# One step of a hybrid decoder: the input projection in another tile order, small steps set between its tiles, the short convolution moved from GpSimd to VectorE

## What is computed

```
x = LN1(alpha*x + 0.5*SwiGLU_a(x))
z = x @ w_in + b_in        # split: conv B, C, h (512 each) | q (512) | kv_cmp, kv_sel, kv_win (256 each) | gates (24)
y_conv = B * conv3(C * h)                       # causal, depthwise, width 3; samples start from state_conv
o = g0*o_cmp + g1*o_sel + g2*o_win              # compressed, selected and window attention, gates g = sigmoid
x = LN2(alpha*x + concat(o, y_conv) @ w_out)
x = LN3(alpha*x + 0.5*SwiGLU_b(x))
```

## Time and profile before

| | us |
|---|---|
| median of 3 runs (lowest, highest) | 1405.66 (1404.45, 1406.14) |
| the profiled execution | 1405.21 |
| its span, first to last instruction | 1403.5 |
| TensorE busy in the span | 1297.5 (92%) |
| VectorE busy | 749.5 (53%) |
| ScalarE busy | 435.4 (31%) |
| GpSimd busy | 280.9 (20%) |
| mean granted clock of TensorE | 0.968 of 2.4 GHz |

### The profile page before, as it was taken

One profiled execution on the slowest core, in us unless ns is written; L12 is line 12 of the kernel. 1 busy time (PEld: TensorE's weight loads), 2 busy tenths in 40 slices (PEclk: granted clock), 3 DMA queues, 4 the chain that ended last, 5 costly groups with the idle time before them and its releaser, 6 DMA issues.

```text
span 1403.5 us, 30051 instructions
## 1 busy us (share of the span) xinstructions
PE 1297.5 (92%) x11917; PEld 1181.4 (84%) x11917; DVE 749.5 (53%) x1178; ACT 435.4 (31%) x814; POOL 280.9 (20%) x272
## 2 busy tenths in 40 slices
PE   6999999999999889999779999497999999999996
PEld 5999999999999779999546666396899999999995
DVE  3686487477748763221546666646444444444446
ACT  3222223132222244222135565314522122222214
POOL 0342044023314312082344332000000000000000
PEclk9999999999999999999789999698999999999999
DMA  4786267246536402331676674131533333323311
GB/s 136 202 225 175 82 176 210 66 132 197 161 92 183 137 24 76 90 90 34 136 256 226 213 239 136 39 89 54 161 106 105 105 104 104 97 85 102 104 60 64
DMA packets 215978, 178.04 MB, mean 127 GB/s; under 512 B 22995, under 2 KB 206466, under 8 KB 215236
## 3 DMA queue, kind: packets, MB, share of 16 engines
q1 hardware_dynamic: 209732, 159.84, 39.2%
q0 software_dynamic: 6144, 16.79, 3.5%
HBM read 172.63 MB, written 8.10 MB: 129 GB/s over the span
## 4 chain that ended last, share of the span: by engine, by line
PE 76%; DVE 12%; ACT 5%; DMA 3%; issue 3%; SPq 1%; POOL 0%; DVEq 0%; ACTq 0%
PE ps L763 44%; PE ps L890 8%; PE ps L817 7%; PE ps L787 4%; DVE dlo L1670 3%; PE ps L1215 2%; DVE glo L1665 2%; DMA w1p<-in_cmp_w_dram 2%; DMA draw<-in_ffa_down_dram 1%; PE ps L1251 1%; PE ps L1186 1%; PE ps L1231 1%; DVE x L1741 1%; ACT ghi L1331 1%; PE ps L1173 1%
## 5 line engine op out<-in xcount | busy, mean ns | idle before, releaser
L763 PE MATMUL ps<-xh,ghi 128*128 128x272 f32 x1904 | 402.0, 293 | 26.2 <-DVE xl L1935 15.7
L763 PE MATMUL ps<-xl,ghi 128*128 128x272 f32 x1904 | 396.4, 290 | 0.0
L763 PE MATMUL ps<-xh,glo 128*128 128x272 f32 x1904 | 394.1, 288 | 0.0
L763 PEld LDWEIGHTS ps<-xh,ghi 128*128 128x128 f32 x1904 | 305.3, 190 | 43.0 <-issue 24.2
L763 PEld LDWEIGHTS ps<-xl,ghi 128*128 128x128 f32 x1904 | 302.0, 190 | 0.0
L763 PEld LDWEIGHTS ps<-xh,glo 128*128 128x128 f32 x1904 | 301.4, 190 | 0.0
L1665 DVE TENSOR_TENSOR glo<-graw,ghi 128x1024 fp32r<-128x1024 f32 x119 | 155.5, 1307 | 107.1 <-ACT ghi L1331 104.9
L696 POOL COPY perm<-landing 128x1024 f32<-128x1024 f32 x64 | 141.0, 2222 | 303.8 <-DMA landing<-in_cache_cmp_kv_dram 303.7
L1741 DVE SCALAR_TENSOR_TENSOR x<-ps,x 128x544 f32<-128x544 f32 x176 | 126.7, 720 | 107.1 <-PE ps L817 106.7
L1800 DVE SCALAR_TENSOR_TENSOR yt<-ps,yt 128x512 f32<-128x512 f32 x88 | 60.6, 691 | 156.6 <-PE ps L890 156.6
L1331 ACT ACTIVATE ghi<-graw 128x1024 fp32r<-128x1024 f32 x119 | 124.8, 1050 | 34.0 <-PE ps L763 30.7
(11 more groups left out here) (335 smaller groups left out, 1478.6 us busy)
## 6 DMA issues: line engine op xcount, KB each, us to landing
landing<-in_cache_cmp_kv_dram SPq DMA_DIRECT2D x256, 128.0 KB, 2.5
page<-in_cache_sel_kv_dram SPq DMA_DIRECT2D x128, 128.0 KB, 4.9
page<-in_cache_sel_kv_dram POOLq DMA_DIRECT2D x128, 128.0 KB, 5.2
graw<-in_ffa_gate_dram SPq DMA_DIRECT2D x22, 512.0 KB, 4.7
graw<-in_ffa_up_dram SPq DMA_DIRECT2D x22, 512.0 KB, 4.4
draw<-in_ffa_down_dram SPq DMA_DIRECT2D x88, 128.0 KB, 2.7
graw<-in_w_in_dram SPq DMA_DIRECT2D x44, 256.0 KB, 3.3
graw<-in_ffb_gate_dram SPq DMA_DIRECT2D x22, 512.0 KB, 3.9
```

What stands on the lines that cost most here:

```text
L763: last = nc.tensor.matmul(out[:, h, 0:HALF], a[:, k, :], b[:, k, h * HALF:(h + 1) * HALF], start=(k == 0 and a is hi and b is xhi), stop=( ...
```

## The change

The projection's tiles are taken in the order keys and values, q, gates, C and h, B. The small steps are made into functions and called on TensorE between the tiles (some in the middle of a tile, behind its fourth chunk, `middle`), and the other engines' programs are set in the matching order; the loops over tiles are written out. `w1p` and its loads go: L1082's step reads `w1`, and the buffers are laid out so that only the convolution's tiles lie over it. The convolution runs on VectorE, one tile of 128 channels at a time, with fused multiply-adds; `conv_ready` is raised once for each of four. GpSimd issues its pages of sample 0 when the last tile is over, as SP does. The gate products' operand `gate_sel` lies in the window buffers, so window loads 0 and 1 wait for these products and come behind the pages of sample 0. In the second feed-forward layer `token_stores` stands ahead of the wait for the norm, and ScalarE waits for these stores before it writes `yt`, which now lies over `kvtok`.

```diff
+ORDER = (*range(ZC + 4, ZC + 10), *range(ZC, ZC + 4), ZC + 10, *range(4, ZC), *range(4))
+AT = {t: (j % 2, j // 2 + 1) for j, t in enumerate(ORDER)}
...
-        w1p = sb("w1p", [128, 2, HD, HD], F32, up)
...
@@ SP @@
                 gate_up(0, 1)
+                token_stores()
                 sp.wait_ge(std_ready, 4)
                 gate_up(1, 1)
                 gate_up(0, 2)
                 down(0)
-                token_stores()
...
-            for t in range(NT):
-                s = t % 2
-                sp.wait_ge(w_lo[s], USES["proj"][s] + t // 2 + ONE)
+            for j, t in enumerate(ORDER):
+                s = j % 2
+                sp.wait_ge(w_lo[s], USES["proj"][s] + j // 2 + ONE)
...
-            sp.wait_ge(w_used[0], USES["proj"][0] + NT // 2 + 1)
-            for c in range(2):
-                for h in range(2):
-                    sp.dma_start(w1p[h * BLK:(h + 1) * BLK, c, :, :], cmp_w1[0, c]).then_inc(q["dma_cmp_w"], 16)
...
-            sp.wait_ge(q["hidx_in_psum"], 1)
+            sp.wait_ge(w_used[0], USES["proj"][0] + NT // 2 + 1)
             sample_loads(0, 0)
-            sp.wait_ge(q["conv_ready"], 1)
+            sp.wait_ge(q["gates_in_psum"], 2)
+            window_load(0, 0)
+            window_load(1, 0)
+            sp.wait_ge(q["conv_ready"], 4)
             sample_loads(1, 0)
...
@@ GpSimd @@
-            taps(slice(0, SEQ), lambda t, tap: (zc[:, 4 + t, 0:SEQ - (2 - tap)], 2 - tap))
-            pool.wait_ge(q["gates_ready"], 1)
-            taps(slice(SEQ, T), lambda t, tap: (sext[:, t, :, tap:tap + NQ], 0))
-            pool.tensor_tensor(yconv[:], zc[:, 0:4, :], zc[:, 8:12, :], ALU.mult).then_inc(q["conv_ready"], 1)
...
-            pool.wait_ge(q["hidx_in_psum"], 1)
+            pool.wait_ge(w_used[0], USES["proj"][0] + NT // 2 + 1)
             page_loads(pool, pages[0], UP, UP, cache_sel, q["dma_page0_pool"])
...
@@ TensorE @@
+            def hidden_prompt():
+                pe.wait_ge(tok_out, QT + 1)
+                pe.wait_ge(q["hid_operand_ready"], 1)
+                for d in range(0, HD, 4):
+                    for c in range(2):
+                        for h in range(2):
+                            part = slice(c * 64 + h * 32, c * 64 + h * 32 + 32)
+                            last = nc.tensor.matmul(ps[part, 0, 0:4 * HD], kd[:, h, c, d:d + 4, :].rearrange("p d x -> p (d x)"),
+                                                    w1[:, c, d:d + 4, :], start=(d == 0), stop=(d == HD - 4))
+                last.then_inc(q["hidx_in_psum"], 1)
...
+            def project(j, middle=None):
+                s = j % 2
+                pe.wait_ge(w_lo[s], USES["proj"][s] + j // 2 + 1 + ONE)
+                if j >= 2:
+                    pe.wait_ge(z_out[s], j // 2)
+                product(ps[:, bank[s]:bank[s] + 2, :], ghi[s], glo[s], xh, xl, KC, (norm_lo, 0) if j == 0 else None,
+                        None if middle is None else lambda c: middle() if c == 4 else None).then_inc(w_used[s], 1)
+
+            project(0)
+            project(1)
+            compressed(GROUPS - 1)
+            for j in range(2, 6):
+                project(j)
...
+            project(6, first_rows)
+            kv_rows(2)
+            kv_rows(3)
+            project(7, lambda: kv_rows(QT))
+            project(8)
+            hidden_prompt()
+            project(9)
+            hidden_sorted()
+            project(10)
+            prompt_blocks()
+            sample_small_scores()
+            project(11)
+            importance()
+            project(12, gates_of_prompt)
+            project(13, selection_rows)
+            for j in range(14, 21):
+                project(j)
+            conv_rows()
+            project(21)
+            project(22)
...
@@ ScalarE @@
+                act.wait_ge(stored, 16 * KV_STORES)
                 rows_begun(0)
...
+            def projected(j):
+                s, i, t = j % 2, j // 2, ORDER[j]
+                dst = zc[:, t:t + 1, :] if t < ZC else zr[:, t - ZC:t - ZC + 1, :]
+                z_result(dst, R_BC + t, s, i, ACT.Sigmoid if t == NT - 1 else ACT.Identity)
...
@@ VectorE @@
+            def convolved(t):
+                dve.wait_ge(z_out[AT[4 + t][0]], AT[4 + t][1])
+                dve.wait_ge(z_out[AT[8 + t][0]], AT[8 + t][1])
+                u, y = zc[:, 4 + t, :], zc[:, 8 + t, :]
+                steps(dve.tensor_tensor(u, u, y, ALU.mult))
+                steps.settle()
+                steps(dve.tensor_copy(sext[:, t, :, 2:2 + NQ], u[:, SEQ:T].rearrange("p (n i) -> p n i", i=NQ)))
+                steps.settle()
+                for tap in (2, 1, 0):
+                    late = 2 - tap
+                    wt = par[:, R_WC + 4 * tap + t:R_WC + 4 * tap + t + 1]
+                    prompt, few = y[:, late:SEQ], y[:, SEQ:T].rearrange("p (n i) -> p n i", i=NQ)
+                    if tap == 2:
+                        steps(dve.tensor_scalar(prompt, u[:, 0:SEQ], wt, None, ALU.mult))
+                        steps(dve.tensor_scalar(few, sext[:, t, :, tap:tap + NQ], wt, None, ALU.mult))
+                    else:
+                        steps(dve.scalar_tensor_tensor(prompt, u[:, 0:SEQ - late], wt, prompt, ALU.mult, ALU.add))
+                        steps(dve.scalar_tensor_tensor(few, sext[:, t, :, tap:tap + NQ], wt, few, ALU.mult, ALU.add))
+                    steps.settle()
+
+            def mixed(t):
+                dve.wait_ge(z_out[AT[t][0]], AT[t][1])
+                dve.tensor_tensor(yconv[:, t, :], zc[:, t, :], zc[:, 8 + t, :], ALU.mult).then_inc(q["conv_ready"], 1)
+
+            for j in range(14, NT - 1):
+                next_low(j)
+                if j >= 16 and j < 20:
+                    convolved(j - 16)
+                if j == 19:
+                    dve.engine_nop().then_inc(q["u_ready"], 1)
+                if j >= 20:
+                    mixed(j - 20)
+            mixed(2)
...
```

More of the change, by code:

```diff
@@ L123 @@
 E_DONE = 4 * FT
+KV_STORES = 3 * QT + 2 + NB
 ROWS_IN = 2 * 16 * FT
@@ L1044, in _ @@
-            last.then_inc(q["s_small_in_psum"], 1)
-            for br in range(2):
-                for nh in range(2):
-                    out = ps[:, 1, (2 * br + nh) * NS:(2 * br + nh + 1) * NS]
-                    nc.tensor.matmul(out, qbd[:, 4 * nh:4 * nh + 4, :].rearrange("p n r -> p (n r)"),
-                                     zr[:, KV0 + 2 + 2 * br, SEQ:T], start=True, stop=False)
-                    last = nc.tensor.matmul(out, identb[:], new_mask[:, nh, :], start=False, stop=True)
@@ L1059, in _ @@
-            pe.wait_ge(q["dma_conv"], 16)
-            for t in range(4):
-                last = nc.tensor.transpose(ps[:, 3, 128 + t * 16:144 + t * 16], crow[:, t * 128:(t + 1) * 128],
-                                           ident[0:16, 0:16])
-            last.then_inc(q["gates_in_psum"], 1)
-            pe.wait_ge(q["pcs_ready"], 1)
-            pe.wait_ge(tok_out, QT + 1)
-            nc.tensor.matmul(ps[:, 4, 0:128], same[:], pcs[:].rearrange("p n b -> p (n b)"), start=True, stop=True)
@@ new lines, in hidden_sorted @@
+            def hidden_sorted():
+                pe.wait_ge(q["hid_operand_ready"], 2)
+                for c in range(2):
+                    for d in range(4):
+                        kept = ident[:, c * 64:c * 64 + 64].rearrange("p (h d x) -> p d h x", h=2, d=4)[:, d]
+                        last = nc.tensor.matmul(ps[c * HD:(c + 1) * HD, 1, 0:2 * QT * G], hidx[:, d * HD:(d + 1) * HD], kept,
+                                                start=(d == 0), stop=(d == 3))
+                last.then_inc(q["hidp_in_psum"], 1)
@@ new lines, in prompt_blocks @@
+            def prompt_blocks():
+                pe.wait_ge(q["hidp_ready"], 1)
+                for g in range(G):
+                    nc.tensor.matmul(ps[g * HD:(g + 1) * HD, 6, 0:8], w2[0:HD, 0, :], hidp[0:HD, :, :, g],
+                                     start=True, stop=True)
+                for g in range(G):
+                    last = nc.tensor.matmul(ps[0:8, 7, g * HD:(g + 1) * HD],
+                                            hidp[HD:128, :, :, g].rearrange("p h a -> p (h a)"), w2[HD:128, 1, :],
+                                            start=True, stop=True)
+                last.then_inc(q["kcp_in_psum"], 1)
@@ new lines, in selection_rows @@
+            def selection_rows():
+                pe.wait_ge(q["sel_ready"], 1)
+                for n in range(NB):
+                    for c in range(CH):
+                        last = nc.tensor.matmul(ps[32 * c:32 * c + 32, 0, n * 16:(n + 1) * 16],
+                                                identb[:, 32 * (n % 4):32 * (n % 4) + 32],
+                                                selneg[:, n // 4, c * 16:(c + 1) * 16], start=True, stop=True)
+                last.then_inc(q["selt_in_psum"], 1)
@@ new lines, in conv_rows @@
+            def conv_rows():
+                pe.wait_ge(q["u_ready"], 1)
+                pe.wait_ge(q["selt_ready"], 1)
```

(26 more changed lines are left out.)

329 lines of the change are left out of this document (139 added, 190 removed).

## The result

Four runs of each kernel give medians of **1382.79 us** after (1382.30 to 1385.38) and 1405.06 us before, a ratio of 0.9849, 95% interval 0.9829 to 0.9869; three of the four runs before are those that the forecast started from.

The account below looks back on a forecast made before the run. TensorE's chain of waits was taken as the bound, with 54.64 us between projection and first key transpose. 54.64 - 15.4 (inserted steps) - 22.0 (tail) = 17.2 us less, from 1405.66 to 1388.5 us; range 1384 to 1398.

Parts of the forecast that it names:

- The window of sample 0: Load queued behind sample 0's pages, issued 11.4 us after the projection's end, landing at 22.5 us, or 15.3 at the low end.
- Inserted steps: Small TensorE steps between projection tiles, each lengthening the projection by its own time: 15.4 us, 20.8 with each dearer end.
- The tail: From the projection's end to the attention's first key transpose: 22.0 us, from ends of 21.4 (compute) and 22.5 (window).
- Rival 1: Ahead of the first key transposes, the window load becomes the wait: 9.2 us gained, 1396.5 us; chance 0.11.
- Rival 2: Between projection tiles, TensorE waits for VectorE or ScalarE: 5 us less gained, 1393.5 us; chance 0.11.
- Rival 3: TensorE's clock falls at the ten places of inserted steps, 2.5 us each: 1413 us; chance 0.05.
- Rival 4: Nothing gained: the wait for `w1p` hid another ending as late, 39.2 us after the projection's end; chance 0.01.
- The range's lower end: 21.0 us gained, 1384.6 us, if the clock held during the softmax (tail 18.2 us) and the window landed early.

Follow-up runs that it names:

- windows_early_filler: Changed kernel plus 16 useless matmuls ahead of the compressed scores' softmax wait, with the first window load between SP's two groups of eight pages: median 1385.81 us.
- gates_early_filler: Changed kernel with gate products between projection tiles 14 and 15, window loads issued behind them, and 16 useless matmuls ahead of the softmax wait: median 1385.70 us.
- same_again_2: The changed kernel a third time, nothing edited, beside the kernel before on the same chip: median 1383.35 us.
- after: The changed kernel as first measured, against the kernel before: median 1382.79 us, ratio 0.9849.
- same_again: The changed kernel run once more, nothing edited: median 1386.28 us.

## Where the prediction was right, and the step that failed

**The mechanism was right.** The order gains; TensorE stays the bound; `po` ends the tail. The window of sample 0 was not as late as forecast: it landed 19.8 us behind E, where the prediction had 22.5. To the key transposes 17.2 us were forecast, and 15.7 to 16.3 were gained.

**Inserted steps, 15.4 us forecast.** In the chain after they are 3.28 us for `kv_rows` and 0.87 for `conv_rows` (forecast 4.1 together), 7.04 for `hidden_prompt` (6.8), 0.83 for `hidden_sorted` (0.9), 1.50 for the small scores (1.25), 1.03 for `importance` and the gates' transposes (1.1), 0.83 for the two short ones (1.2): 15.4 us. The projection grew by 149.59 - 133.10 = 16.5. The 1.1 us that the sum lacks were put at nothing: most of them, 0.9 us, are the restarts of the products behind the five steps of small matmuls, 0.1 to 0.2 us each.

**The tail, 22.0 us forecast: 22.3.** Gate products 2.79 (2.65 forecast), the short products 1.97 (1.1), the score transposes 1.64, at half clock already (1.09), and from their end to the keys 13.7 (14.4).

**Rival 1** did not come: the window of sample 0 landed 2.5 us ahead of `po`. The room behind `po` is small all the same: in `windows_early_filler` and `gates_early_filler` a page ended the wait. **Rival 2** did not come: TensorE waited for `glo` 0.3 us, ahead of the first tile, and not between the tiles. The price of VectorE's fused operations, which the prediction did not find in the trace, is there: in the last norm of the kernel before, L1884 takes 749 ns on 128x512 from SBUF, and the new ones took 750. **Rival 3** did not come: the clock was 1.00 from 531 to 681 us, transposes included. The Trainium skill (TensorE: Matmul & The Clock Gate, Part 4: PE-mode transpose) says that transposes do not count as busy in the same way; this trace, with 30 of them between products from 565.3 to 574.6 us, shows no fall. The longest group among them is 1.31 us, with products on both sides; what a longer group does, no run here shows. The one fall seen at an inserted step, in `gates_early_filler`, stood behind 24 small products, and cost 1.5 us. **Rival 4** is out.

**The step that failed** is the last one, how the sum became a time and a range. "The profiled execution took 1405.21 us against a median of 1405.66 us of the three runs, 0.03% off, so the gain carries over unscaled" took three runs within 1.7 us for the kernel's spread. In 47 runs it spans 1399.16 to 1409.77 us around a mean of 1403.17 us, so the base was 2.5 us too high. The range's lower end, 1384, was built from bounds of terms alone and holds nothing for the runs: for the stage ahead of P, 4.4 us between two executions of the same code, nor for the clock at the first sample (1.6 us) and in the output projection (1.4 us). The median of four runs after, 1382.79, lies 1.9 us under the mean of 13, and that of before 1.9 us over the mean of 47. Those 3.8 us are most of the 5.1 by which forecast and result differ, and they are the luck of few runs.

A second step fell short: behind L1215 the sum put nothing, because "nothing there is edited but the place of the window loads". Against 16.0 us to the keys, the three executions after gained 17.2 us on average to the last group (845.4 - 828.2), and 1.1 of these 1.2 us lie in the first sample, where the clock held in two of the three. The output projection took 50.3 us on average in both. That 17.2 is just the number forecast is therefore luck as well: the restarts cost 1.1 us that were not in the sum, and the first sample gave as much back. From these 17.2 to the 18.5 us of the means it is 1.3, plus or minus 1.6, which can't be told from chance.

## What to carry to other kernels

The length of a piece in the chain of waits is not what its removal gains: look for the engine's own idle time there (3.30 of 21.54 us), then sum what is left behind it. A step set into a stream of products costs its own time and, behind small matmuls, a restart of up to 0.2 us; it is worth it where it took the engine's waits with it. Where several ends lie within five microseconds, mending one of them brings the next one forward: no such change here gained more than 3.1 us to the keys. A gain of 1% is forecast with the spread of the runs in its range.

## What was not expected of the hardware

- Two profiled executions of code that is the same up to P differ by 4.4 us there, with waits for weights of 16.8 and 12.0 us.
- Where the granted clock falls differs between executions of one kernel: at the first sample in `same_again_2`, not in `after` and `same_again`. In the old order it fell there in all three executions.
- A filler meant to raise the clock ran at half clock itself (5.1 us for what took 3.8 us in `windows_early_filler`) and only moved the fall to the next stage.
